# A two-layer encoder in float32 on one core: the first projection's weight groups in three rounded products instead of one float32 product, and the last chunk of each FFN in another order

## The chip, the cores and the metric

The kernel runs on one core of one Trainium2 chip. The metric is the time of one execution on the device in microseconds (us); lower is better.

## The reference

256 tokens of width 2048 go through two layers. Layer 0 mixes tokens with a convolution module, layer 1 with multi-head latent attention; each mixer is followed by a gated FFN (SwiGLU) of width 5632. All arithmetic is float32. What the change touches is the convolution module and the two FFNs:

```python
def swiglu(h, w_gate, w_up, w_down):
    return (jax.nn.silu(h @ w_gate) * (h @ w_up)) @ w_down

def conv_module(h, w_pw1, b_pw1, w_dw, b_dw, ln_g, ln_b, w_pw2, b_pw2):
    u = h @ w_pw1 + b_pw1                 # 2048 -> 4096
    a, gate = jnp.split(u, 2, axis=-1)
    v = a * jax.nn.sigmoid(gate)
    v = depthwise_causal_conv(v, w_dw, width=31) + b_dw
    v = jax.nn.silu(layernorm(v, ln_g, ln_b))
    return v @ w_pw2 + b_pw2
...
h = h + conv_module(rmsnorm(h), ...)      # layer 0; layer 1: h + mla(rmsnorm(h), ...)
h = h + swiglu(rmsnorm(h), ...)
```

## The kernel before

**Rounded products.** TensorE multiplies float32 slowly, and numbers rounded to the type fp32r fast. So a weight group (1 MB: four row tiles of 128 by 512 columns) is split in two: ScalarE writes the rounded high part `w_hi` from `raw` (`hi`, L665; `f_hi`, L793), VectorE writes the rest `w_lo = raw - w_hi` (`lo`, L981; `f_lo`, L986). The activations are split the same way into `x_hi` and `x_lo`, and a product is the sum of three: high times high, high times low, low times high (`product`, L1493).

**The rings.** `raw`, `w_hi` and `w_lo` have four slots each. A load into a `raw` slot (SyncE's queue, L485, L460, L514) waits until the low part of the slot's earlier group is made. ScalarE's high part waits until TensorE has used the slot's earlier group.

**The first projection.** It is done in eight halves; half s holds 256 value and 256 gate columns, as four groups j = 0 to 3 of four row tiles (`channel_half`, L1577). Groups 0 and 1 (`WHOLE = 2`) are multiplied in plain float32 straight from `raw`, with activations `x_f`; the load of their slot waits for TensorE itself. Groups 2 and 3 are split, but without VectorE: ScalarE writes `w_hi`, and then minus `raw`, rounded, into `w_lo` (`hi_and_negative`, L674), and a transfer issued by GpSimd adds `raw` to it (`conv_low`, L587). For the first group row of the second projection (`G_PW2` to `G_PW2 + 3`) the transfers do it too.

**What the other engines do in a half.** ScalarE takes the sigmoid of the gate (`gate_sigmoid`, L715), and multiplies 10 of the 31 taps of the convolution (`products`, L726); GpSimd sums those (`conv_sums`, L593). VectorE multiplies value and gate (L1086) and does the other 21 taps of two channel tiles, the two tiles in turn (L1096, L1101), adds GpSimd's sum (L1107) and takes row statistics (L1120). TensorE transposes the result of half s - 2 in half s (`conv_rows`, L1612). In the last half 12 taps are done by TensorE with diagonal matrices `diag_last` (L712, `conv_rows_last`, L1625); ScalarE writes these 24 matrices before half 0's sigmoid. After it come a layernorm, transposes, SiLU (`silu`, L1140) and the second projection (`square`, L1651).

**The FFN.** The hidden width is done in 11 chunks of 512. A chunk c from 1 to 10 takes 15 weight groups, in the order of L98. Seven are Strassen sums (Q1 to Q7, 12 multiplications each), four are plain (G2, G3, U2, U3, 24 each), and four (D0 to D3, 24 each) are the down projection of the chunk before. `hidden` transposes the gated activations of a chunk and splits them into `a_hi` and `a_lo`. The slot of `w_hi` and `w_lo` is the group's number modulo 4; for the last four groups, the down projection of chunk 10 (numbers 158 to 161), it is 0 to 3:

```python
def f_w(q):
    return q % RING if q < F_LAST else q - F_LAST
```

ScalarE's `f_hi` of a group waits until TensorE has used the group before it in that slot. In chunk 10 the order before is ..., D3, Q2, G2, Q4, G3, U2 (number 156), U3 (157), then `hidden(10)`, then groups 158 to 161. The order of each engine is written out by hand in `ffn(l)`: on VectorE the end of a chunk is `gate_mul(c)` (L1254), low part of the next chunk's group 0, then 1, with `up_mul(c)` (L1261) between them, 2, and `hidden(c)` (L1246).

Of the kernel before, what the change touches and what calls it, by code (L numbers as in the profile page):

```python
# [28 lines left out]
F32 = mybir.dt.float32  # L29
# [23 lines left out]
PE_TAPS_LAST = 12  # L53

# [5 lines left out]
WHOLE = 2  # L60
SPLIT = KG - WHOLE

# [16 lines left out]

G_ADDED = G_PW2 + RING  # L80
# [18 lines left out]
DOWN = (D0, D1, D2, D3)  # L99
F_CHUNK = 15  # L100
# [3 lines left out]
F_RAW = {Q1: 0, Q5: 0, Q6: 0, Q4: 0, Q3: 1, Q7: 1, D0: 4, D1: 2, D2: 3, D3: 4, Q2: 2, G2: 3, G3: 4, U2: 2, U3: 3}  # L104


def f_pos(c, p):
    return F_FIRST + F_CHUNK * (c - 1) + p


def f_part(q):
    return (q - F_FIRST) % F_CHUNK


def f_raw(q):

    if q < F_FIRST:
        return q % RING
    return F_RAW[f_part(q)] if q < F_LAST else q - F_LAST
# [61 lines left out]
def encoder(nc, x, positions, attn_norm_g, ffn_norm_g, final_norm_g, conv_w_pw1, conv_b_pw1, conv_w_dw,  # L181
# [3 lines left out]
    with ctx:  # L185
# [15 lines left out]

        with nc.sbuf_tensor("x_f", [P, WHOLE * GK, S], F32) as x_f:
            pass
# [114 lines left out]
        xf_done = sem("xf_done")  # L318
# [4 lines left out]
        glu_done = sem("glu_done")  # L323
        conv_step = sem("conv_step")
# [57 lines left out]
        def in_float32(g):  # L382
            return g < G_PW2 and g % KG < WHOLE

        def split_no(g):

            return SPLIT * (g // KG) + g % KG - WHOLE if g < G_PW2 else SPLIT * HALVES + g - G_PW2

        def wait_lo(eng, g, i=None, per=0):
            if KG <= g < G_ADDED:  # L390
                eng.wait_ge(lo_added[g % RING], 16 * (g // KG if g % KG >= WHOLE else 1))
            else:
                eng.wait_ge(lo_dve, val(split_no(g) + 1 if g < KG else SPLIT + g - G_ADDED + 1, i, per))

# [9 lines left out]
        def wait_f_used(eng, l, q):  # L404
            eng.wait_ge(f_used, F_ALL * l + q + 1)

# [23 lines left out]
        def norm_counts(n):  # L430

            return KT * n - WHOLE * GK

# [17 lines left out]
        def _(sp):  # L451
# [50 lines left out]
            def ffn_loads(l):  # L502
# [23 lines left out]
                for c in range(1, FC):  # L526
                    for p in (D3, Q2, G2):
                        part(c, p)
                    if c < FC - 1:
                        part(c + 1, Q3)  # L530
                    for p in (G3, U2, U3):
                        part(c, p)
                    if c < FC - 1:
                        part(c + 1, Q1)
                        for p in (D0, D1, D2):
                            part(c + 1, p)
                for n in range(CC):
                    f_load(F_LAST + n, w_of(l, DOWN[n], FC))
            ffn_loads(0)
# [37 lines left out]
        def _(pool):  # L577
# [9 lines left out]
            def conv_low(g):  # L587

                slot = g % RING
                pool.wait_ge(neg_done, split_no(g) - SPLIT + 1)  # L590
                pool.dma_start(hi32(w_lo[:, slot, :]), raw[:, slot, :], accum_op=ALU.add).then_inc(lo_added[slot], 16)

            def conv_sums(s):  # L593
# [3 lines left out]
                for n in range(1, PROD_TAPS[s]):  # L597
                    pool.wait_ge(prod_done, 2 * (PROD_TAP[s] + n) + 2)
# [5 lines left out]
                    if n == 2 and s < HALVES - 1:  # L604
                        conv_low(G_PW1 + KG * (s + 1) + KG - 1)
# [51 lines left out]
        def _(act):  # L657
# [44 lines left out]
            for j in range(WHOLE, KG):  # L702
                hi(G_PW1 + j)
                for k in range(GK * j, GK * j + GK, 2):
                    act.wait_ge(xt_done, k + 2 - WHOLE * GK)
# [3 lines left out]
            act.wait_ge(vec_done, 3)  # L709
            for mm in range(2):  # L710
                for w in range(PE_TAPS_LAST):
# [3 lines left out]
            def gate_sigmoid(s):  # L715

                u = s % 2
                act.wait_ge(group_used, G_PW1 + KG * s + KG)
                if s >= 2:
                    act.wait_ge(glu_done, 2 * (s - 1))  # L720
                for mm in range(2):
                    col = KT + 2 * s + mm
                    act.activation(glu_sig[:, 2 * u + mm, :], ps[:, 2 * u + 1, S * mm:S * mm + S], ACT.Sigmoid,
                                   bias=bias1_col[:, col:col + 1]).then_inc(glu_sig_done, 1)

            def products(s, n0, n1):  # L726

                u = s % 2
                for n in range(n0, min(n1, PROD_TAPS[s])):
                    w = prod_tap0(s) + n  # L730
                    if n == 0 and s >= 2:
                        act.wait_ge(conv_tr, TT * (s - 1))
                    elif n > 0 and PROD_ADD[s] + n > PROD_SLOTS:
                        act.wait_ge(prod_added, PROD_ADD[s] + n - PROD_SLOTS)
                    elif n > 0:
                        act.wait_ge(out_added, TT)
                    for mm in range(2):
                        m, tile = 2 * u + mm, 2 * s + mm
                        act.wait_ge(glu_done, tile + 1)
                        dst = acc[:, m, :] if n == 0 else prod_slot(s, n)[:, S * mm:S * mm + S]  # L740
                        act.activation(dst, vbuf[:, m, w:w + S], ACT.Copy, scale=tap_col[:, w, tile:tile + 1]
                                       ).then_inc(prod_done, 1)
# [9 lines left out]
            for s in range(HALVES):  # L752
                g = G_PW1 + KG * (s + 1)
                if s == HALVES - 1:
                    hi_and_negative(g)
                    hi_and_negative(g + 1)
                hi_and_negative(g + 2)
                gate_sigmoid(s)
                products(s, 0, 3)
                hi_and_negative(g + 3)  # L760
                if s > 0:
                    rows_out(s - 1)
                products(s, 3, TAPS)
# [50 lines left out]
            def ffn(l):  # L814

                def gate_sig(c):

                    for t in range(TT):
                        if c > 0 and t == 0:
                            act.wait_ge(tile0_done, 2 * chunk_no(l, c) + 1)  # L820
                        else:
                            wait_f_used(act, l, KG - 1 if c == 0 else f_pos(c, G3))
# [3 lines left out]
                def hidden(c):  # L826

                    for b in range(2):
                        act.wait_ge(ff_tr, 2 * (FC * l + c) + b + 1)
                        act.activation(a_hi[:, 0, 2 * b:2 * b + 2, :].rearrange("p k s -> p (k s)"), ps[:, 4 + b, :],  # L830
                                       ACT.Copy).then_inc(ahi_done, 1)

                def parts_hi(c, *parts):
                    for p in parts:
                        f_hi(l, f_pos(c, p))

# [8 lines left out]
                for c in range(1, FC):  # L845
# [4 lines left out]
                    wait_f_used(act, l, f_pos(c, Q5))  # L850
                    act.activation(q5, ps[:, 3, :], ACT.Copy).then_inc(q5_done, 1)
                    parts_hi(c, Q6, D2, Q7, D3, Q2, G2)
                    wait_f_used(act, l, f_pos(c, Q7))
                    act.activation(q167, ps[:, 1, :], ACT.Copy).then_inc(q167_done, 1)
                    parts_hi(c, Q4, G3, U2, U3)
                    parts_hi(c + 1, 0)
                    gate_sig(c)
                    if l == 1 and c == FC - 1:
                        wait_f_lo(act, l, f_pos(c, G3))
                        act.dma_start(row_bc[:, :], final_norm_g.rearrange("(a d) -> a d", a=1).to_broadcast([P, D])  # L860
                                      ).then_inc(final_g_in, 16)
                    parts_hi(c + 1, 1, 2)
                hidden(FC - 1)
                f_hi(l, F_ALL - 1)
# [107 lines left out]
        def _(dve):  # L972
# [53 lines left out]
            def first_norm(gain):  # L1026
# [17 lines left out]
                for k in range(WHOLE * GK):  # L1044
                    scaled(k, x_f[:, k, :]).then_inc(xf_done, 1)
                dve.wait_ge(sq_act, 1)
                for j in range(WHOLE, KG):
                    for k in range(GK * j, GK * j + GK):
                        scaled(k, x_t[:, S * k:S * k + S]).then_inc(xt_done, 1)
                    lo(G_PW1 + j)  # L1050
                    for k in range(GK * j, GK * j + GK, 2):
                        dve.wait_ge(xhi_done, k + 2 - WHOLE * GK)
# [4 lines left out]
                dve.tensor_copy(bias1_col[:, :], ps[:, 6, 0:2 * KT]).then_inc(vec_done, 1)  # L1057
                dve.tensor_copy(tap_col[:, :, :].rearrange("p w t -> p (w t)"), ps[:, 7, 0:TAPS * KT]).then_inc(vec_done, 1)
# [20 lines left out]
            def conv_half(s):  # L1079

                u = s % 2
                dve.wait_ge(group_used, G_PW1 + KG * s + KG)
                for mm in range(2):
                    m, tile = 2 * u + mm, 2 * s + mm
                    dve.wait_ge(glu_sig_done, tile + 1)
                    dve.scalar_tensor_tensor(vbuf[:, m, HALO:], ps[:, 2 * u, S * mm:S * mm + S],  # L1086
                                             bias1_col[:, tile:tile + 1], glu_sig[:, m, :],
                                             ALU.add, ALU.mult).then_inc(glu_done, 1)
                w0 = dve_tap0(s)
                bank = [ps[:, 6 + u, S * mm:S * mm + S] for mm in range(2)]  # L1090
                for w in range(w0, TAPS):
                    for mm in range(2):
                        m, tile = 2 * u + mm, 2 * s + mm
                        if w == w0:
                            dve.wait_ge(glu_done, tile + 1)
                            dve.tensor_scalar(bank[mm], vbuf[:, m, w:w + S], tap_col[:, w, tile:tile + 1],  # L1096
# [888 lines left out]
```

## Time and profile before

| | us |
|---|---|
| median of 3 runs (2070.03 to 2072.25) | 2071.71 |
| the profiled execution, its own time | 2071.21 |
| span of the profiled execution | 2069.4 |
| TensorE busy | 2010.9 |
| VectorE busy | 1421.9 |
| ScalarE busy | 1054.8 |
| GpSimd busy | 226.1 |

The span is what the instructions of the profile cover; the time has some 1.8 us around it. Engines are called PE (TensorE), PEld (its weight loads), DVE (VectorE), ACT (ScalarE), POOL (GpSimd) and SP (SyncE) in the profile; a q behind a name is an engine's instruction queue. PEclk is the share of full speed that TensorE's clock was granted. A float32 matmul stands in the profile as two records, a rounded one as one.

### The profile page before, as it was taken

The page shows a single profiled execution, that of the slowest core. Times are in us where ns is not written, and L with a number is a line of the kernel's source. Part 1 is how long each engine was busy: PE and PEld are TensorE (multiplying, and loading weights), DVE is VectorE, ACT ScalarE, POOL GpSimd, SP SyncE. Part 2 cuts the span into 40 slices and gives each one's busy share as a digit, 9 for nine tenths or more (in the row PEclk, how much of TensorE's full clock was granted, in tenths as well). Part 3 has the DMA queues.
Part 4 walks back from the last instruction along what each step waited for, and adds up shares of the span by engine and source line. Part 5 has one row for each costly group of instructions (what it writes and reads, how often), then busy time and mean ns, then how long its engine had stood idle before and what let it go on. Part 6 is the DMA issues. An engine that isn't in the chain of part 4 may idle for free.

```text
span 2069.4 us, 24296 instructions
## 1 busy us (share of the span) xinstructions
PE 2010.9 (97%) x9814; PEld 1705.5 (82%) x9814; DVE 1421.9 (69%) x1605; ACT 1054.8 (51%) x1020; POOL 226.1 (11%) x191
## 2 busy tenths in 40 slices
PE   8899899999999999999989999999999999999996
PEld 7898878888888888888878998888888888888885
DVE  4777676777766777667667775477766767766764
ACT  4566763545454555455445554355455445554543
POOL 0455400000000000000001000000000000000001
PEclk9999999999999999999999999999999999999998
DMA  7888946699889989898744534568988999889981
GB/s 234 240 227 234 263 143 214 169 279 258 227 224 259 268 267 236 216 260 245 243 143 138 158 122 160 191 177 270 251 217 240 253 274 262 224 227 262 263 244 61
DMA packets 254081, 457.51 MB, mean 221 GB/s; under 512 B 18452, under 2 KB 60188, under 8 KB 251164
## 3 DMA queue, kind: packets, MB, share of 16 engines
q1 hardware_dynamic: 207648, 349.73, 48.3%
q0 software_dynamic: 44832, 102.77, 28.7%
q10 hardware_dynamic: 1500, 3.61, 0.5%
q8 instruction: 71, 1.16, 0.2%
q14 instruction: 30, 0.25, 0.0%
HBM read 435.10 MB, written 2.10 MB: 211 GB/s over the span
## 4 chain that ended last, share of the span: by engine, by line
PE 85%; DVE 5%; DMA 5%; ACT 3%; issue 1%; POOL 0%; SPq 0%; ACTq 0%; DVEq 0%; POOLq 0%
PE ps L1496 82%; DVE w_lo L988 2%; DMA raw<-in_conv_w_pw_dram 2%; DMA w_lo<-raw 1%; DMA raw<-in_ffn_w_up_dram 1%; PE ps L1719 1%; POOL scratch L603 0%; PE ps L1920 0%; PE ps L1921 0%; PE ps L1901 0%; ACT w_hi L801 0%; DMA resid<-in_x_dram 0%; ACT w_lo L677 0%; ACT diag_last L712 0%; DVE x_lo L1015 0%
## 5 line engine op out<-in xcount | busy, mean ns | idle before, releaser
L988 DVE TENSOR_TENSOR w_lo<-raw,w_hi 128x2048 fp32r<-128x2048 f32 x264 | 601.5, 2287 | 279.0 <-ACT w_hi L801 278.7
L801 ACT ACTIVATE w_hi<-raw 128x2048 fp32r<-128x2048 f32 x264 | 500.9, 1914 | 488.3 <-PE ps L1496 197.1
L1496 PE MATMUL ps<-w_hi,x_hi 128*128 128x512 f32 x1328 | 517.9, 390 | 1.1 <-DVE x_lo L1015 0.9
L1496 PE MATMUL ps<-w_hi,x_lo 128*128 128x512 f32 x1328 | 516.7, 389 | 0.0
L1496 PE MATMUL ps<-w_lo,x_hi 128*128 128x512 f32 x1328 | 516.7, 389 | 0.0
L1496 PE MATMUL ps<-w_hi,a_hi 128*128 128x512 f32 (+1 forms) x768 | 294.5, 384 | 2.5 <-DVE a_lo L1250 2.5
L1496 PE MATMUL ps<-w_lo,a_hi 128*128 128x512 f32 (+1 forms) x768 | 293.9, 383 | 0.0
L1496 PEld LDWEIGHTS ps<-w_hi,x_hi 128*128 128x128 f32 x1328 | 249.3, 188 | 53.9 <-DVE x_lo L1015 1.4
L1496 PE MATMUL ps<-w_hi,a_lo 128*128 128x512 f32 (+1 forms) x768 | 293.6, 382 | 0.0
L1496 PEld LDWEIGHTS ps<-w_hi,x_lo 128*128 128x128 f32 x1328 | 249.3, 188 | 52.1
L1496 PEld LDWEIGHTS ps<-w_lo,x_hi 128*128 128x128 f32 x1328 | 249.3, 188 | 51.3
L622 POOL DMA_DIRECT2D raw<-in_ffn_w_up_dram x60 | 77.1, 1285 | 1255.1 <-DVE w_lo L988 1255.1
L672 ACT ACTIVATE w_hi<-raw 128x2048 fp32r<-128x2048 f32 x73 | 138.5, 1910 | 147.8 <-PE ps L1496 74.3
L1496 PEld LDWEIGHTS ps<-w_hi,a_hi 128*128 128x128 f32 x768 | 145.6, 190 | 31.7 <-DVE w_lo L988 3.5
L1496 PEld LDWEIGHTS ps<-w_hi,a_lo 128*128 128x128 f32 x768 | 145.6, 190 | 28.0
L1496 PEld LDWEIGHTS ps<-w_lo,a_hi 128*128 128x128 f32 x768 | 145.6, 190 | 27.7
L801 ACT ACTIVATE w_hi<-row_bc 128x2048 fp32r<-128x2048 f32 x60 | 115.2, 1919 | 92.7 <-PE ps L1496 92.7
L983 DVE TENSOR_TENSOR w_lo<-raw,w_hi 128x2048 fp32r<-128x2048 f32 x55 | 125.5, 2291 | 40.8 <-ACT w_hi L672 40.6
L988 DVE TENSOR_TENSOR w_lo<-row_bc,w_hi 128x2048 fp32r<-128x2048 f32 x60 | 137.0, 2284 | 4.6 <-ACT w_hi L801 4.5
L1496 PE MATMUL ps<-w_hi,s_hi 128*128 128x512 f32 x320 | 126.4, 395 | 0.0
L1496 PE MATMUL ps<-w_hi,s_lo 128*128 128x512 f32 x320 | 124.8, 390 | 0.0
L1496 PE MATMUL ps<-w_lo,s_hi 128*128 128x512 f32 x320 | 124.5, 389 | 0.0
(210 smaller groups left out, 2323.8 us busy)
## 6 DMA issues: line engine op xcount, KB each, us to landing
raw<-in_ffn_w_gate_dram SPq DMA_DIRECT2D x68, 1024.0 KB, 9.5
raw<-in_ffn_w_up_dram SPq DMA_DIRECT2D x68, 1024.0 KB, 7.5
raw<-in_ffn_w_up_dram POOLq DMA_DIRECT2D x60, 1024.0 KB, 9.0
raw<-in_ffn_w_down_dram SPq DMA_DIRECT2D x48, 1024.0 KB, 6.0
row_bc<-in_ffn_w_down_dram SPq DMA_DIRECT2D x40, 1024.0 KB, 8.8
raw<-in_conv_w_pw_dram SPq DMA_DIRECT2D x64, 512.0 KB
raw<-in_ffn_w_gate_dram POOLq DMA_DIRECT2D x20, 1024.0 KB, 9.8
row_bc<-in_ffn_w_gate_dram SPq DMA_DIRECT2D x20, 1024.0 KB, 6.4
```

The source lines that it names most:

```text
L622: pool.dma_start(f_raw_tile(l, q).rearrange("p (k n) -> p k n", k=GK), w_of(l, p, c), accum_op=ALU.add).then_inc(f_added[f_raw(q)], 16)
L672: act.activation(w_hi[:, slot, :], raw[:, slot, :], ACT.Copy).then_inc(hi_done, 1)
L801: act.activation(f_w_tile(w_hi, l, q), f_raw_tile(l, q), ACT.Copy).then_inc(f_hi_done, 1)
L983: dve.tensor_tensor(w_lo[:, g % RING, :], raw[:, g % RING, :], hi32(w_hi[:, g % RING, :]), ALU.subtract).then_inc(lo_dve, 1)
L988: dve.tensor_tensor(f_w_tile(w_lo, l, q), f_raw_tile(l, q), hi32(f_w_tile(w_hi, l, q)), ALU.subtract).then_inc(f_lo_done, 1)
L1496: ins = pe.matmul(dst, lhsT, rhs, start=first and n == 0, stop=last and n == len(pairs) - 1, skip_group_check=skip)
L1719: ins = pe.transpose(ps[:, 4 + b, S * kk + P * t:S * kk + P * t + P], ff_h[:, t, P * m:P * m + P], ident[:, :])
```

## The change

- All groups of the first projection but group 0 of half 0 are now split. In each half from 1 on, the low parts of groups 0 and 1 are made by VectorE and those of groups 2 and 3 by transfers, as before (`ADDED_FROM = 2`). Loads into the slots of groups 0 and 1 now wait for the low part and not for TensorE. `x_hi` and `x_lo` are made for all 16 row tiles, in the order of groups 1, 2, 3, 0.
- The low parts of `G_PW2` to `G_PW2 + 3` are made by VectorE: one before `silu(0)`, three inside the SiLU loop.
- ScalarE writes the diagonal matrices four per half in halves 1 to 6, and a small sigmoid early.
- GpSimd issues both transfers of a half before it starts its sums.
- In half 7 groups 2 and 3 are multiplied for channel tile 0 first and then for tile 1; sigmoid, taps and products are done for tile 0 and then for tile 1, no longer in turn.
- In chunk 10 of each FFN, D2 and D3 move behind U3, with `hidden(10)` between them; Q2 stands before Q7, and Q4 behind G3. `hidden(10)` has its own slot of `a_hi` and `a_lo` and uses PSUM banks 0 and 1.

```diff
-WHOLE = 2
-SPLIT = KG - WHOLE
+FIRST_ORDER = (1, 2, 3, 0)
+ADDED_FROM = 2
...
+ORDER_LAST = (Q1, Q3, Q5, D0, D1, Q6, Q2, Q7, G2, G3, Q4, U2, U3, D2, D3)
...
 def f_pos(c, p):
-    return F_FIRST + F_CHUNK * (c - 1) + p
+    return F_FIRST + F_CHUNK * (c - 1) + (ORDER if c < FC - 1 else ORDER_LAST).index(p)
...
         def in_float32(g):
-            return g < G_PW2 and g % KG < WHOLE
+            return g == G_PW1
...
@@ GpSimd
             for s in range(HALVES):
-                if s == HALVES - 1:
-                    for j in range(WHOLE):
-                        conv_low(G_PW2 + j)
-                    conv_low(G_PW2 + WHOLE)
-                else:
-                    conv_low(G_PW1 + KG * (s + 1) + WHOLE)
+                if s < HALVES - 1:
+                    for j in range(ADDED_FROM, KG):
+                        conv_low(G_PW1 + KG * (s + 1) + j)
                 conv_sums(s)
-            conv_low(G_PW2 + KG - 1)
...
@@ ScalarE, a half
+            for s in range(HALVES - 1):
+                g = G_PW1 + KG * (s + 1)
+                hi(g + 1)
+                hi_and_negative(g + 2)
+                for mm in range(2):
+                    gate_sigmoid(s, mm)
+                hi_and_negative(g + 3)
+                products(s, 0, 3)
+                if s > 0:
+                    rows_out(s - 1)
+                products(s, 3, PROD_TAPS[s])
+                if s < HALVES - 2:
+                    hi(g + KG)
+                if s > 0:
+                    last_diagonals(s - 1)
...
@@ VectorE, a half but the last
+                    gated(0)
+                    gated(1)
+                    lo(G_PW1 + KG * (s + 1) + 1)
+                    for w in range(w0, TAPS):
+                        tap(w, 0)
+                        tap(w, 1)
+                    if s < HALVES - 2:
+                        lo(G_PW1 + KG * (s + 2))
...
@@ ScalarE, chunk 10
+                        parts_hi(c, G3, Q4, U2, U3)
+                        gate_sig(c)
+                        parts_hi(c, D2, D3)
+                        f_hi(l, f_next(c, 0))
...
+                    f_hi(l, f_next(c, 1))
...
                 hidden(FC - 1)
-                f_hi(l, F_ALL - 1)
+                for n in (2, 3):
+                    f_hi(l, F_LAST + n)
...
@@ VectorE, chunk 10
+                        gate_mul(c)
+                        parts_lo(c, D2, D3)
+                        f_lo(l, f_next(c, 0))
+                        up_mul(c)
+                        f_lo(l, f_next(c, 1))
+                        hidden(c)
+                        add(2, f_pos(c, D2))
+                        f_lo(l, f_next(c, 2))
...
@@ TensorE, chunk 10
                     plain(c, U2, 2, 2)
                     plain(c, U3, 2, 3)
+                    if c == FC - 1:
+                        down(c - 1, 2, f_pos(c, D2))
+                        hidden(c)
+                        down(c - 1, 3, f_pos(c, D3))
...
-                        if block_no >= 2:
+                        if block_no >= 2 or c == FC - 1:
                             pe.wait_ge(out_added, added + TT * CC * c + block_no - 3)
```

## Rows read from the trace of the kernel before

**Rows 1.** The page: the chain that ended last, share of the span by line.

```profile
PE ps L1496 82%; DVE w_lo L988 2%; DMA raw<-in_conv_w_pw_dram 2%; DMA w_lo<-raw 1%; DMA raw<-in_ffn_w_up_dram 1%; PE ps L1719 1%; POOL scratch L603 0%; PE ps L1920 0%; PE ps L1921 0%; PE ps L1901 0%; ACT w_hi L801 0%; DMA resid<-in_x_dram 0%; ACT w_lo L677 0%; ACT diag_last L712 0%; DVE x_lo L1015 0%
```

**Rows 2.** Windows, by stage: length, engines' busy us, granted clock, transfers' busy share, GB/s.

```profile
43.10:77.40 34.30, 28.02 (x162) 25.81 (x161) 18.19 (x46) 23.77 (x38) 14.33 (x12) 0.90 0.70 185
...
155.80:181.70 25.90, 25.90 (x166) 24.03 (x165) 18.86 (x48) 16.78 (x28) 13.31 (x11) 1.00 0.93 242
181.70:211.20 29.50, 27.53 (x167) 25.62 (x165) 18.86 (x48) 18.28 (x29) 13.28 (x11) 0.94 0.90 240
...
1043.70:1054.00 10.30, 7.00 (x20) 5.57 (x21) 8.01 (x7) 3.47 (x4) 0.00 (x0) 0.50 0.66 217
```

**Rows 3.** TensorE's timeline in the halves: start, duration, records, idle time before.

```profile
31.00 0.28 PE L1496 MATMUL ps<-x_lo,w_hi 128*128 128x256 f32 x1
...
36.39 0.28 PE L1496 MATMUL ps<-x_lo,w_hi 128*128 128x256 f32 x1
...
69.40 0.58 PE L1496 MATMUL ps<-x_hi,w_hi 128*128 128x256 f32 x1 [4.82 <-DMA w_lo<-raw]
...
129.68 7.07 PE L1496 MATMUL ps<-x_f,raw 128*128 128x256 f32 x32
162.67 0.60 PE L1621 MATMUL ps<-ident,scratch 128*128 128x128 f32 x4
...
203.85 0.43 PE L1496 MATMUL ps<-x_hi,w_hi 128*128 128x256 f32 x1 [1.97 <-DMA w_lo<-raw]
```

**Rows 4.** The half from 129.7 to 155.8, instructions by line and shape.

```profile
L1101 DVE SCALAR_TENSOR_TENSOR ps<-scratch,tap_col,ps 128x256 f32<-128x256 f32 x40 | 15.8, 483 | 0.0
...
L603 POOL TENSOR_TENSOR scratch<-scratch,row_bc 128x512 f32<-128x512 f32 x9 | 11.6, 1286 | 2.9 <-ACT row_bc L741 1.9
...
L672 ACT ACTIVATE w_hi<-raw 128x2048 fp32r<-128x2048 f32 x2 | 3.8, 1904 | 9.5 <-DMA raw<-in_conv_w_pw_dram 9.5
```

**Rows 5.** Transfers in the half from 155.8 to 181.7, by queue (q1 loads, q0 the additions).

```profile
GB/s 350 348 346 98 3 8 0 0 202 202 202 202 202 202 202 101 101 55 345 387 369 389 302 215 240 215 202 215 234 136 378 383 383 354 350 353 343 359 350 361
...
q1 hardware_dynamic: 4174, 4.14, 48.5%
q0 software_dynamic: 288, 2.10, 43.6%
```

**Rows 6.** VectorE's timeline ahead of half 0 and in the SiLU loop.

```profile
38.38 4.49 DVE L1075 TENSOR_TENSOR resid<-resid,row_bc 128x2048 f32<-128x2048 f32 x2
...
266.89 0.69 DVE L1144 TENSOR_TENSOR scratch<-scratch 128x512 f32<-128x512 f32 x1 [2.74 <-ACT scratch L784]
```

**Rows 7.** TensorE's timeline behind the last half.

```profile
241.21 12.58 PE L1496 MATMUL ps<-diag_last,scratch 128*128 128x128 f32 x96 [3.65 <-DVE scratch L1086]
257.32 1.16 PE L1496 MATMUL ps<-ident,scratch 128*128 128x128 f32 x8 [3.53 <-DVE scratch L1107]
...
269.90 0.47 PE L1496 MATMUL ps<-w_hi,x_hi 128*128 128x512 f32 x1 [0.20 <-DVE x_lo L1152]
```

**Rows 8.** The chain at the end of the first FFN.

```profile
1034.93 5.45 PE ps L1496 x24
...
1040.47 1.92 ACT w_hi L801
...
1044.62 1.40 DVE scratch L1268 x2
...
1048.97 13.52 PE ps L1496 x48
```

**Rows 9.** VectorE in chunk 10 of the first FFN, around Q6 and Q7.

```profile
1002.69 0.69 DVE L1304 TENSOR_TENSOR scratch<-scratch,ps 128x512 f32<-128x512 f32 x1
1003.41 0.70 DVE L1306 TENSOR_TENSOR ps<-ps,scratch 128x512 f32<-128x512 f32 x1
```

**Rows 10.** GpSimd's issue of a transfer, beside VectorE idle and beside a low part.

```profile
398.98 1.29 POOL L622 DMA_DIRECT2D raw<-in_ffn_w_up_dram  x1 [1.94 <-DVE w_lo L988]
...
472.44 1.28 POOL L622 DMA_DIRECT2D raw<-in_ffn_w_up_dram  x1 [7.73 <-DVE w_lo L988]
```

More of the change, by code:

```diff
@@ L118, in f_raw @@
         return q % RING
[L119 removed]
+    if q >= F_LAST:
+        return q - F_LAST
+    return (F_RAW_LAST if in_last(q) else F_RAW)[f_part(q)]
 def f_w(q):
@@ L708, in _, with last_diagonals @@
             act.dma_start(row_bc[:, :], conv_b_pw2[0:1, :].to_broadcast([P, D])).then_inc(bias2_in, 16)
-            act.wait_ge(vec_done, 3)
-            for mm in range(2):
-                for w in range(PE_TAPS_LAST):
+            act.activation(esum[:, 0:1], ident[:, 0:1], ACT.Sigmoid).then_inc(warm, 1)
+            def last_diagonals(part):
+                for n in range(part * DIAG_PART, (part + 1) * DIAG_PART):
+                    w, mm = n // 2, n % 2
                     act.activation(diag_last[:, mm, w, :], ident[:, :], ACT.Copy,
@@ L744, in rows_out @@
+            def products(s, n0, n1):
+                for n in range(n0, n1):
+                    for mm in range(2):
+                        product_of(s, n, mm)
             def rows_out(s):
@@ L1089, in conv_half @@
[L1089 to L1102 removed]
+                last = s == HALVES - 1
@@ new lines, in conv_half, with gated @@
+                w0 = dve_tap0(s)
+                steps = TAPS - w0
+                bank = [ps[:, 6 + u, S * mm:S * mm + S] for mm in range(2)]
+                def gated(mm):
+                    tile = 2 * s + mm
+                    dve.wait_ge(glu_sig_done, tile + 1)
+                    dve.scalar_tensor_tensor(vbuf[:, 2 * u + mm, HALO:], ps[:, 2 * u + mm, 0:S],
+                                             bias1_col[:, tile:tile + 1], glu_sig[:, 2 * u + mm, :],
+                                             ALU.add, ALU.mult).then_inc(glu_done, 1)
@@ new lines, in tap @@
+                def tap(w, mm):
+                    m, tile = 2 * u + mm, 2 * s + mm
+                    if w == w0:
+                        dve.wait_ge(glu_done, tile + 1)
+                        dve.tensor_scalar(bank[mm], vbuf[:, m, w:w + S], tap_col[:, w, tile:tile + 1],
+                                          vec_col[:, R_BDW + tile:R_BDW + tile + 1],
+                                          ALU.mult, ALU.add).then_inc(conv_step, 1)
+                        return
+                    dve.wait_ge(conv_step, DVE_STEP[s] + (steps * mm + w - w0 if last else 2 * (w - w0) + mm - 1))
+                    dve.scalar_tensor_tensor(bank[mm], vbuf[:, m, w:w + S], tap_col[:, w, tile:tile + 1],
+                                             bank[mm], ALU.mult, ALU.add).then_inc(conv_step, 1)
@@ new lines, in conv_half @@
+                if last:
+                    for mm in range(2):
+                        gated(mm)
+                        for w in range(w0, TAPS):
+                            tap(w, mm)
+                else:
+                    gated(0)
+                    gated(1)
+                    lo(G_PW1 + KG * (s + 1) + 1)
+                    for w in range(w0, TAPS):
+                        tap(w, 0)
+                        tap(w, 1)
+                    if s < HALVES - 2:
+                        lo(G_PW1 + KG * (s + 2))
@@ L1584, in channel_half @@
                     g = G_PW1 + KG * s + j
-                    if j < WHOLE:
+                    if in_float32(g):
                         pe.wait_ge(raw_in[g % RING], LANDED * (g // RING + 1))
-                        w = w_rows(raw, g % RING)
                     else:
                         wait_lo(pe, g)
-                        wh, wl = w_rows(w_hi, g % RING), w_rows(w_lo, g % RING)
-                    if s == 0 and j < WHOLE:
-                        pe.wait_ge(xf_done, GK * (j + 1))
+                    if s == 0 and j == 0:
+                        pe.wait_ge(xt_done, GK)
@@ new lines, in channel_products @@
+            def channel_products(s, j, tiles):
+                slot = (G_PW1 + KG * s + j) % RING
+                w, wh, wl = w_rows(raw, slot), w_rows(w_hi, slot), w_rows(w_lo, slot)
+                for kk in range(GK):
+                    k = GK * j + kk
+                    for m in tiles:
+                        cols = slice(P * m, P * m + P)
+                        if in_float32(G_PW1 + KG * s + j):
+                            pairs = [(w[:, kk, cols], x_t[:, S * k:S * k + S])]
+                        else:
+                            pairs = [(wh[:, kk, cols], x_hi[:, k, :]), (wh[:, kk, cols], x_lo[:, k, :]),
+                                     (wl[:, kk, cols], x_hi[:, k, :])]
+                        ins = product(ps[:, 2 * (s % 2) + m % 2, S * (m // 2):S * (m // 2) + S], pairs,
+                                      k == 0 and m < 2, k == KT - 1, skip=True)
+                return ins
```

343 lines of the change are left out of this document (198 added, 145 removed).

## The prediction

> **What bounds it now.** I read the page first, for where the time is: TensorE is busy 2010.9 us of 2069.4 (the table), and 82% of the chain that ended last is its multiplications [rows 1]. So a change pays only where it takes work from TensorE or a gap out of its row. Then I read the windows by stage [rows 2], TensorE's timeline [rows 3, 7] and the chain around each gap [rows 8].
>
> In the halves of the first projection TensorE hardly waits: the half from 155.8 lasts 25.9 us, the clock is granted in full, and transfers are busy 93% beside it. A float32 group is 32 records in 7.07 us [rows 3]. A rounded one is 48 multiplications; 45 of them start between 31.00 and 36.39, 0.12 us each, so 5.76 us [rows 3]. Two of each and the transposes of 0.6 make 26.2. Two halves stand out: the one from 43.1 takes 34.3, the one from 181.7 takes 29.5 [rows 2]; both wait for a transfer into `w_lo` (4.82 and 1.97 us) [rows 3] and then run at a lower clock. Behind the last half TensorE idles 3.65 us, does the diagonal taps in 12.6, idles again, and starts the second projection at 269.9 [rows 7].
>
> At each FFN's end U3 stops at 1040.4. The chain goes on over ScalarE's high part of group 159, VectorE's low part and `up_mul` to 1046.0, and the next multiplication starts at 1048.97 [rows 8]. The clock is at 0.50 from 1043.7 to 1054.0, so 48 multiplications take 13.5 us [rows 2, 8].
>
> **The change, part by part.**
>
> *Half 0.* One float32 group becomes rounded: 7.07 to 5.76, so half 1 begins at 43.1 - 1.2 = 41.9. The low parts of groups 1, 2, 3 lie under group 0's multiplications.
>
> *Half 1.* Its floor is four groups, 23.05 us, against 34.3. The long wait goes: ScalarE no longer writes 24 matrices ahead of the rounded copies, and transfers are issued before the sums. VectorE gets later: the row it adds to the residual is requested behind one more high part. Its 4.49 us of adds began at 38.4 [rows 6]; I take 40.1 (38.4 to 42 are the ends), so it takes up half 0 at 44.6. The low part of group 8 comes 21.8 later (18.86 less 1.5 of adds and statistics, plus two low parts of 2.2; DVE's busy time of [rows 2]), at 66.4, while TensorE wants it at 41.9 + 23.05 = 64.95. Half 2 begins at 66.5, before at 77.4.
>
> *Halves 2 to 7.* TensorE's floor is 4 x 5.76 + 0.6 = 23.65. The others come close. VectorE: 18.86 [rows 2] + 2 x 2.2 = 23.3. ScalarE: 16.78 [rows 2] + two high parts of 1.8 (1904 ns, overlapping by 0.1) [rows 4] + four matrices of 0.3 = 21.6. Transfers: (48.5% + 43.6%) of 25.9 = 23.9 [rows 5], 24.1 with the bytes that slid into the next half. GpSimd's nine sums of 1.29 [rows 4] have room. So transfers become the tightest. What orders them: a load waits until the earlier addition in its slot has landed, the addition waits for ScalarE's two copies of the group, and ScalarE stands in order with the sigmoid. I follow one half from its start at 0: additions issued at about 0 and 5.6 (sigmoids 0.9, two copies 3.7, issue 0.9), loads behind low parts at -1 and 4, the other two loads behind the additions. The queue is never empty as long as an addition ends before the load queued beside it. Bounds for a half are 23.65 (nothing late) and 26 (2 us of idle transfers, if both end together). I take 24.4: 24.1 and 0.3 for starts. Half 7 ends at 66.5 + 6 x 24.4 = 212.9, before at 241.21 - 3.65 = 237.6 [rows 7]: **-24.7 us**.
>
> *Behind half 7.* The taps of a tile now follow one another, and each reads what the one before wrote. In turn, 40 take 15.8 us, 0.39 each, at a duration of 0.48 [rows 4]. Dependent steps of 0.69 start 0.72 apart [rows 9], so a dependent tap costs 0.51, and 14 of them 7.2. VectorE is free of half 6 just before half 7 ends (0), finishes tile 0 at 7.3, gates tile 1, and is through at 15.1, with the adds at 15.9. TensorE's diagonal taps (12.6) and GpSimd's four sums end by then. Before, the same matmuls started 257.32 - 237.56 = 19.8 behind the half [rows 7]: **-3.9**. The low parts in the SiLU loop: the first fits into the idle 2.74 [rows 6]; the one behind block 0 makes block 1 some 1.2 later, of which TensorE feels **+0.5**. Bounds 0 and +3.
>
> *FFN, chunk 10, middle.* Q7 needs `mix_q1_q6`, which had D2's 5.44 us as cover and now has Q2's 2.7. VectorE's queue put its second step at 1002.7 [rows 9]; it ends at 1003.4, and TensorE is there at 1002.3: 1.1, and 0.2 for G2's low part behind it. **+1.3** per layer.
>
> *FFN, chunk 10, end.* One would read D2 and D3 as cover for the gaps before and behind `hidden(10)`. But look at who holds the slots of `w_hi`. Groups 158 and 159 have slots 0 and 1, as numbers 156 and 157 do. These were U2 and U3; now they are D2 and D3. ScalarE's high part of 158 waits until D2 is used, VectorE makes its low part *before* `up_mul`, and the transposes wait for `up_mul`. So behind D2 stands the same chain as before behind U3: 1.9 + 2.2 + 1.4, 5.7 us of idle [rows 8]. Then D3 runs, and the high part of 159, ahead of ScalarE's copy into `a_hi`, waits until D3 is used. Behind D3: high part 1.9, low part 2.2, two `a_lo` 1.2, and the first residual add of D2 0.6, because block 0 now waits for it: 6.0 us of idle. The clock falls 3.3 us into a gap and is back 10.3 later [rows 2, 8]. Taken over as it stands here, the first gap, transposes and D3 take 16.1 us for 6.3 of work (9.8 lost), the second loses 6.0 and 7.5 us at half speed, 9.8. Together 19.6, with the middle 20.9. Before: from 1040.4 to 1062.5 22.1 us for 11.8 of work [rows 8], 10.3 lost. So +10.6 per layer, **+21.2** in both. Bounds: +12 for both if the clock falls once only, +24.
>
> Sum: -24.7 - 3.9 + 0.5 + 21.2 = -6.9. The profiled execution's time is 2071.2 (span 2069.4 and 1.8 around it), 0.5 under the median: 2064.3 for it, 2064.8 for the median. I say **2065 us**.
>
> **Rivals.**
> 1. *Transfers set the halves.* If loads and additions share the engines so that both end together, the next load leaves them idle for some 2 us and a half takes 25.7 to 26. In [rows 5] the second addition runs beside a load at 302 to 389 GB/s for five slices and then alone at some 215, so they do mix. Six halves at 26 instead of 24.4 give 2065 + 9.6 = 2074.6, no change. From 26.4 a half on, it is slower. That point is reached if waits of 2 us as at 203.85 [rows 3] come back, each with its half clock: a half of 27 gives 2081. For it: VectorE, ScalarE and transfers all above 88% of the half. Against: both waits of before came from a late issue, which is now early. [...]
> 2. *The FFN ends are covered after all* (I misread the slots): both lose only the 1.3 in the middle. -2 x 9.0 instead of +21.2: 2026.
> 3. *The clock falls once per FFN end* or the second gap is half as long: +12 instead of +21: 2056.
>
> **Chances.** My forecast, 2059 to 2069: 0.50. Rival 1: 0.27, of which 0.14 within 0.2% (4.1 us, about what a measurement of this kernel can tell) and 0.13 slower. Rival 2: 0.07. Rival 3: 0.16. Of my forecast some 0.06 lies within 4.1 us of before. Faster 0.67, same 0.20, slower 0.13. The range leaves out rival 2 and the far end of rival 1: 2054 to 2077.
>
> **What would show it.** Half 1 has no wait of 4.8 us, and half 2 begins near 66.5. Halves 2 to 6 are 24 to 25 us apart; waits in them are for `w_lo<-raw`. The matmuls of the last conv rows start some 16 us behind half 7. In each FFN two gaps near 6 us stand around D3, the first ended by `up_mul`, the second by VectorE, and the granted clock falls twice. Wrong would be: no gap behind D2 (rival 2), or halves above 25.5 (rival 1).

## The result and the profile after

The changed kernel takes 2059.38 us (median of 5 runs, 2054.65 to 2062.48); the kernel before took 2070.73 (5 runs, 2069.95 to 2072.25). The ratio is 0.9936, with a 95% interval of 0.9920 to 0.9952: 0.64% faster. The profiled execution took 2054.65 us, the fastest of the five, with a span of 2052.8; before it was 2069.4, so the two traces differ by 16.6 us where the medians differ by 11.4. The runs also scatter more than before, 7.8 us against 2.3.

Where the 16.6 us are, from the two traces: the second projection of the convolution module ends at 328.66 instead of 357.20 (-28.5); from there to the residual transposes at the first FFN's end it is 710.88 us instead of 705.28 (+5.6); the attention part keeps its 281.0; the rest, with the second FFN, grows from 725.9 to 732.25 (+6.35).

**The halves.** Windows over the halves, cut at about their starts, columns as in [rows 2]:

```profile
42.00:66.00 24.00, 21.79 (x180) 21.38 (x179) 24.00 (x49) 20.07 (x29) 13.51 (x11) 1.00 0.94 240
65.00:89.00 24.00, 23.57 (x197) 23.36 (x196) 22.78 (x49) 21.28 (x35) 13.38 (x11) 1.00 0.97 262
...
137.50:161.50 24.00, 23.63 (x197) 23.43 (x197) 23.01 (x51) 21.89 (x35) 13.39 (x11) 1.00 0.98 264
...
186.00:206.50 20.50, 17.30 (x145) 17.09 (x143) 19.11 (x45) 17.14 (x32) 12.19 (x11) 1.00 0.98 256
```

The half from 43.1, 34.3 us in [rows 2], is now some 24, and the transfers have gone from 0.93 to 0.98 of a half. The sigmoids of halves 1 and 6 start at 67.95 and 188.75, five halves at 24.16. What repeats from one half to the next is seen in the chain, one turn of it (start, duration, what):

```profile
77.05 0.39 SPq L510
...
77.48 11.24 DMA raw<-in_conv_w_pw_dram
...
88.77 1.80 issue
90.57 1.90 ACT w_lo L705
92.47 0.29 issue
92.76 8.26 DMA w_lo<-raw
...
101.04 0.39 SPq L510
```

A load lands, ScalarE makes the high part and the negative copy, the addition lands, and only then the next load of that slot is issued: 23.99 us, 19.5 of them two transfers. TensorE is not in it. A share of 0.98 does not mean that the transfers never pause. The half from 137.5 to 161.5 in 40 slices of 0.6 us:

```profile
GB/s 367 215 22 43 131 328 384 387 432 316 218 218 218 191 205 205 205 15 225 377 374 333 425 299 205 196 201 241 246 242 203 171 348 369 386 362 213 271 379 382
```

At 22 and 43 GB/s (138.7 to 139.9) the load has landed and ScalarE still makes the copies, up to 140.60, that the addition waits for. Behind the last half the chain reads:

```profile
193.51 12.99 DMA w_lo<-raw
...
206.54 10.38 PE ps L1603 x72
216.91 0.44 PE ps L1743 x4
217.35 10.72 PE ps L1603 x96
...
228.10 0.72 PE ps L1603 x4
```

The last addition needs 13 us from issue to landing and TensorE waits 3.24 for it; behind this wait the clock is at 0.50 for 3.4 us (207.3 to 210.7). Half 7 ends at 216.9, and the last matmuls of the convolution rows start 11.2 us behind it, right behind the diagonal taps.

**The FFN's end.** TensorE's waits in the whole kernel (line, releaser: us in total, times, longest), and the chain at the end of the first FFN, which answers to [rows 8]:

```profile
PE ps L1603 <- DVE resid L1365: 12.5, 2, 6.2
PE ps L1844 <- DVE scratch L1357: 11.4, 2, 5.7
PE ps L1642 <- DMA resid<-in_x_dram: 8.1, 2, 5.9
PE ps L1603 <- DMA w_lo<-raw: 7.6, 6, 3.2
```

```profile
969.97 36.87 PE ps L1603 x161
...
1006.91 1.92 ACT w_hi L850
...
1009.00 2.07 issue
1011.07 1.41 DVE scratch L1357 x2
...
1012.52 1.97 PE ps L1844 x8
1014.49 6.35 PE ps L1603 x24
...
1020.92 1.92 ACT w_hi L850
...
1022.86 2.29 DVE w_lo L1054
1025.16 1.20 DVE a_lo L1339 x2
1026.35 0.60 DVE resid L1365
...
1027.05 12.49 PE ps L1603 x48
```

The gap of 5.7 us behind U3 has become a gap of 5.7 behind D2, and a second one of 6.2 stands behind D3, step by step as forecast. The clock does not follow the forecast. Windows, column PEclk:

```profile
1009.40:1016.30 6.90, 3.78 (x13) 3.39 (x14) 3.07 (x3) 0.00 (x0) 0.00 (x0) 0.51 0.46 152
1016.30:1023.10 6.80, 4.52 (x20) 3.40 (x19) 0.24 (x1) 2.18 (x2) 0.00 (x0) 1.00 0.00 0
1023.10:1029.90 6.80, 2.85 (x7) 2.30 (x8) 6.80 (x7) 4.30 (x4) 0.00 (x0) 0.50 0.44 154
```

It falls twice, to 1.2 of 2.4 GHz, but is back after 6.8 us each time, in [rows 2] after 10.3.

### The profile page after: what moved, and what is told of

Same layout as the page of the kernel before. It is cut to its first block, busy times and chain, and to the rows that moved or that the text cites. A ratio compares the mean times of both kernels' runs of the same rounds, so it can differ in the third digit from the quotient of the medians.

```text
span 2052.8 us, 24901 instructions
## 1 busy us (share of the span) xinstructions
PE 1991.1 (97%) x10054; PEld 1696.8 (83%) x10054; DVE 1468.4 (72%) x1628; ACT 1078.4 (53%) x1036; POOL 223.5 (11%) x187
## 4 chain that ended last, share of the span: by engine, by line
PE 83%; DMA 8%; DVE 4%; ACT 2%; issue 2%; SPq 0%; POOL 0%; ACTq 0%; DVEq 0%; POOLq 0%
PE ps L1603 80%; DMA raw<-in_conv_w_pw_dram 4%; DMA w_lo<-raw 3%; DVE w_lo L1054 2%; PE ps L1844 1%; DMA raw<-in_ffn_w_up_dram 1%; ACT w_lo L705 1%; ACT w_hi L850 1%; PE ps L2066 0%; PE ps L2067 0%; PE ps L2047 0%; DMA resid<-in_x_dram 0%; SPq L510 0%; PE ps L1653 0%; DVE w_lo L1049 0%
## 5 line engine op out<-in xcount | busy, mean ns | idle before, releaser
L1054 DVE TENSOR_TENSOR w_lo<-raw,w_hi 128x2048 fp32r<-128x2048 f32 x264 | 601.6, 2288 | 290.2 <-ACT w_hi L850 289.8
L850 ACT ACTIVATE w_hi<-raw 128x2048 fp32r<-128x2048 f32 x264 | 500.6, 1915 | 482.8 <-PE ps L1603 218.8
L700 ACT ACTIVATE w_hi<-raw 128x2048 fp32r<-128x2048 f32 x88 | 167.0, 1912 | 95.0 <-PE ps L1603 73.2
L1049 DVE TENSOR_TENSOR w_lo<-raw,w_hi 128x2048 fp32r<-128x2048 f32 x74 | 169.0, 2290 | 40.9 <-ACT w_hi L700 40.6
L1603 PEld LDWEIGHTS ps<-w_hi,a_lo 128*128 128x128 f32 x768 | 145.8, 190 | 28.1
L1603 PE MATMUL ps<-x_hi,w_hi 128*128 128x256 f32 (+1 forms) x512 | 147.1, 287 | 7.6 <-DMA w_lo<-raw 7.6
L1603 PE MATMUL ps<-x_hi,w_lo 128*128 128x256 f32 (+1 forms) x512 | 145.5, 284 | 0.0
L1603 PE MATMUL ps<-x_lo,w_hi 128*128 128x256 f32 (+1 forms) x512 | 145.4, 284 | 0.0
```

The costliest lines, as they stand in the source:

```text
L700: act.activation(w_hi[:, slot, :], raw[:, slot, :], ACT.Copy).then_inc(hi_done, 1)
L850: act.activation(f_w_tile(w_hi, l, q), f_raw_tile(l, q), ACT.Copy).then_inc(f_hi_done, 1)
L1049: dve.tensor_tensor(w_lo[:, g % RING, :], raw[:, g % RING, :], hi32(w_hi[:, g % RING, :]), ALU.subtract).then_inc(lo_dve, 1)
L1054: dve.tensor_tensor(f_w_tile(w_lo, l, q), f_raw_tile(l, q), hi32(f_w_tile(w_hi, l, q)), ALU.subtract).then_inc(f_lo_done, 1)
L1603: ins = pe.matmul(dst, lhsT, rhs, start=first and n == 0, stop=last and n == len(pairs) - 1, skip_group_check=skip)
```

## The experiments

Eleven kernels ran. The kernel before had a median of 2071.3 us beside the first four, 2073.0 beside the next four and 2071.6 beside the last three (9 runs each), so kernels of different groups are compared with up to 2 us of doubt.

**Each part alone.** The first kernel has the whole change but its FFN part; the second has the FFN part only.

> The changed kernel with the order of chunk 10 of both FFNs as before (D2 and D3 in front, one hidden(10) behind U3). Theory: the FFN part of the change costs 5.6 us in layer 0 and 6.4 in layer 1 (the profiles before and after, from the end of the second projection or of the output projection on), so this is 12 us faster than the changed kernel: 2047 (ratio to before 0.9886). If the forecast's size of 21 were right and the profile after lucky, 2038. Rival, the FFN part helps and the profile misleads: above 2059.

> The kernel before with only the new order of chunk 10 of both FFNs. Theory: two gaps near 6 us per layer in place of one, 12 us slower than before: 2083. With the clock low for 10.3 us behind each gap, as forecast: 2092. Rival, D2 and D3 cover the gaps: 2053.

Measured: 2044.22 us (2042.25 to 2045.14), ratio 0.9864 [0.9849, 0.9879], and 2084.63 (2084.28 to 2089.78), ratio 1.0069 [1.0055, 1.0082]. The first projection gives 27.1 us, 3 more than expected (2047), and the FFN part takes 13.4 back; together they make 13.7 us faster, between the 11.4 of the medians and the 16.6 of the spans. Taken between the first kernel and the changed one, the FFN part costs 15.2 us in the medians; the traces before and after give 12.0. The FFN part alone makes the kernel slower, and both gaps are in its trace at the same sizes as in the changed kernel:

```profile
PE ps L1563 <- DVE resid L1325: 12.5, 2, 6.2
PE ps L1789 <- DVE scratch L1317: 11.4, 2, 5.7
```

The first of these kernels also bears on the length of the low clock, for its two FFN ends are the same instructions in the same order, each with a gap of 5.7 us, as in the kernel before. Windows of it:

```profile
1020.80:1027.60 6.80, 4.76 (x15) 3.82 (x16) 5.71 (x6) 2.99 (x3) 0.00 (x0) 0.50 0.78 237
1027.60:1037.30 9.70, 9.70 (x45) 7.97 (x44) 4.62 (x4) 1.92 (x1) 0.00 (x0) 1.00 0.48 161
2003.80:2014.10 10.30, 6.33 (x18) 5.04 (x19) 8.68 (x7) 4.14 (x4) 0.00 (x0) 0.50 0.00 0
```

One end has 6.8 us at the low clock, the other 10.3. The length is not fixed by the gap and the instructions around it, then: the same ones come with either.

**Which wait makes the two gaps.** The third kernel moves one line on VectorE, the fourth covers both gaps:

```diff
 parts_lo(c, D2, D3)
-f_lo(l, f_next(c, 0))
 up_mul(c)
+f_lo(l, f_next(c, 0))
 f_lo(l, f_next(c, 1))
```

```diff
 # VectorE
 parts_lo(c, D2, D3)
-f_lo(l, f_next(c, 0))
 up_mul(c)
-f_lo(l, f_next(c, 1))
+f_lo(l, f_next(c, 0))
 hidden(c)
 add(2, f_pos(c, D2))
+f_lo(l, f_next(c, 1))
 f_lo(l, f_next(c, 2))
 # ScalarE
-    f_hi(l, f_next(c, 1))
     if c < FC - 1:
+        f_hi(l, f_next(c, 1))
         f_hi(l, f_next(c, 2))
 hidden(FC - 1)
-for n in (2, 3):
+for n in (1, 2, 3):
     f_hi(l, F_LAST + n)
```

> The changed kernel; on VectorE in chunk 10 up_mul now stands in front of the low part of group 158. Theory of the slots: the first gap of each layer (5.7 us, slow transposes 1.1, low clock in D3 0.9) goes, the one behind D3 stays: 2 x 7.7 = 15 us less than the changed kernel, 2044. Rival, the gap is due to up_mul's own wait for U3 or to the transposes: no change, 2059.

> As the run with up_mul first, and on ScalarE and VectorE hidden(10) stands in front of group 159's high and low part (VectorE: up_mul, low part of 158, hidden, adds of D2, low parts of 159 and 160). Theory: both gaps go and the clock stays up in both layers, 2 x 15.5 = 31 us less than the changed kernel: 2028. Rival, the second gap only moves (low part of 159 late, D(10, 1) waits 4 us): 2036. Rival, loads of groups 158 to 161 are late: above 2040.

Measured: 2043.51 us (2039.92 to 2045.07), ratio 0.9861 [0.9845, 0.9876], and 2029.31 (2028.13 to 2034.18), ratio 0.9799 [0.9786, 0.9813]. So the first gap of both layers is worth 16 us and the second 14, each with its stretch at the low clock. In the fourth kernel the same place reads, in the chain:

```profile
1010.14 0.87 PE ps L1844 x8
1011.02 5.47 PE ps L1603 x24
...
1016.57 1.93 ACT w_hi L850
...
1018.52 4.49 DVE w_lo L1054 x2
1023.01 0.61 DVE resid L1365
...
1023.75 5.71 PE ps L1603 x24
1029.47 0.87 PE ps L1653 x8
```

The transposes take 0.87 us instead of 1.97, the multiplications 5.47 instead of 6.35, and of both gaps one wait of 1.7 us remains, ahead of the last 24, at the full clock. This version beats both kernels: 30 us under the changed one, 42 under the one before. The experiments below start from it, and "the covered version" is this one.

**What sets the halves.** Half the bytes of each addition, and 6 of VectorE's 21 taps left out:

```diff
-pool.dma_start(hi32(w_lo[:, slot, :]), raw[:, slot, :], accum_op=ALU.add)
+pool.dma_start(hi32(w_lo[:, slot, 0:GK * CH // 2]), raw[:, slot, 0:GK * CH // 2], accum_op=ALU.add)
```

```diff
 def dve_tap0(s):
-    return prod_tap0(s) + PROD_TAPS[s]
+    return prod_tap0(s) + PROD_TAPS[s] + (6 if s < HALVES - 1 else 0)
```

> The version with both FFN ends covered, but each adding transfer of the first projection moves only the first half of its columns (the other half of those low parts stays the negative copy, so the product is wrong there). VectorE, ScalarE, GpSimd and TensorE have the same work. Theory (transfers set halves 2 to 7): the halves fall from 24.2 to TensorE's own 23.65 us, 3.3 us in six halves, and the wait of 5.0 us in half 7 goes, of which VectorE, 3.1 us ahead there, lets through 3.1: 2029.3 - 6.4 = 2023, bounds 2020 and 2026; the waits of TensorE for w_lo<-raw fall from 8.7 us to under 2. Rival (VectorE or ScalarE sets the halves, the transfers only end last by chance): 2028 to 2031, halves still 24.2 apart.

> The version with both FFN ends covered, but VectorE leaves out 6 of its 21 taps for each of the two tiles of halves 0 to 6 (those terms of the depthwise convolution are missing): 12 x 0.39 = 4.7 us less for VectorE in each half. Theory (transfers set the halves, VectorE only follows): 2029, bounds 2027 and 2031, halves 24.0 to 24.5 apart, the additions and their waits where they were. Rival (VectorE, at 22.4 to 23.1 of 24 us, sets the halves, through the low parts that free the slots for the loads): 2023 or less, halves at 23.65.

Measured: 2020.68 us (2019.62 to 2022.70), ratio 0.9752 [0.9736, 0.9768], and 2027.77 (2027.62 to 2032.51), ratio 0.9790 [0.9773, 0.9807]. The same half in either:

```profile
137.50:161.50 24.00, 24.00 (x202) 24.00 (x202) 23.71 (x52) 22.11 (x35) 13.39 (x11) 1.00 0.80 225
```

```profile
137.50:161.50 24.00, 23.54 (x196) 23.34 (x196) 18.66 (x38) 21.57 (x34) 15.31 (x12) 1.00 1.00 263
```

With half the additions TensorE is never idle in it and the halves are 23.52 us apart (sigmoids at 65.52 and 183.14), against 24.35 in the covered version. With VectorE at 18.7 of 24 us they are 24.14 apart, where the changed kernel, with all its taps, has 24.16: nothing gained, and the time is the covered version's within the doubt between groups. Transfers set the halves, VectorE does not. ScalarE's two copies are in the same loop (some 4 us of the 24) and no run shortens them, so how much of a half they hold is not shown. The first result is 8.6 us under the covered version where 6.4 was expected: 0.83 us per half came, not 0.55, since four groups need 23.5 us of TensorE and not 23.65.

**The wait in half 7.** In the covered version it is 5.0 us. The low part of the last group goes to VectorE, after 7 of its taps:

```diff
 for w in range(w0, TAPS):
     tap(w, 0)
     tap(w, 1)
+    if s == HALVES - 2 and w == w0 + 6:
+        lo(G_PW2 - 1)
```

> The version with both FFN ends covered, and the low part of the last group of half 7 made by VectorE after 7 of its taps instead of by the adding transfer that landed 13.9 us after its issue. TensorE's wait of 5.0 us in half 7 goes. Theory (VectorE is next in line): its taps of half 6 end 2.2 us later, so of its 3.1 us of idle time 0.9 is left to gain: the last matmuls of the convolution rows start at 229.3, before 230.2, and the time is 2028.4, bounds 2027 and 2031. Rival (the wait is worth its 5.0 us and the half clock behind it, 1.7): 2022 to 2024.

Measured: 2029.02 us (2027.11 to 2031.13), ratio 0.9791 [0.9774, 0.9807]: no gain, as the theory had it. TensorE's wait of 5.0 us for the addition is gone. In its place TensorE waits 2.5 us for VectorE ahead of and among the transposes and the diagonal taps, and 2.4 us ahead of the last matmuls, which start at 229.8 instead of 230.2.

**The order of the last taps.** The last half's 28 taps alternate again between the tiles:

```diff
-for mm in range(2):
-    gated(mm)
-    for w in range(w0, TAPS):
-        tap(w, mm)
+gated(0)
+gated(1)
+for w in range(w0, TAPS):
+    tap(w, 0)
+    tap(w, 1)
```

> The version with both FFN ends covered, but VectorE's 28 taps of half 7 alternate between the two tiles again, both gated first, while TensorE and ScalarE keep the order tile by tile. Theory: the taps start when tile 1 is there (219.5 instead of 214.3) and take 28 x 0.39 = 10.9 us instead of two times 7.3 and a gate: the adds end near 231.5 instead of 230.2, and the time is 2030.8, bounds 2029 and 2032. Rival (tile by tile is worth the 3.9 us that the prediction gave to the stretch behind half 7): 2033 or more.

Measured: 2029.90 us (2029.21 to 2031.53), ratio 0.9794 [0.9779, 0.9810]. That is the covered version's time within its scatter: tile by tile is worth at most 1 to 2 us there. In the trace the last matmuls start at 230.4, 12.8 behind the half (217.6), against 11.2 in the covered version.

**What removed the long wait of half 1.** The matrices go back ahead of half 0's copies; or the second addition goes back behind two sums:

```diff
+for part in range(HALVES - 2):
+    last_diagonals(part)
 for s in range(HALVES - 1):
     g = G_PW1 + KG * (s + 1)
     hi(g + 1)
 ...
-    if s > 0:
-        last_diagonals(s - 1)
```

```diff
 # in conv_sums, behind each sum
+if n == 2 and s < HALVES - 1:
+    conv_low(G_PW1 + KG * (s + 1) + KG - 1)
 ...
-for j in range(ADDED_FROM, KG):
+for j in range(ADDED_FROM, KG - 1):
     conv_low(G_PW1 + KG * (s + 1) + j)
```

> The version with both FFN ends covered, but ScalarE writes the 24 diagonal matrices of the last half ahead of half 0's copies, as the kernel before did, instead of four per half. 24 x 0.3 = 7.3 us on ScalarE near 35, of which 2.2 fall into its idle time: the two additions of half 1 are issued some 5 us later. Theory (the long wait in half 1 came from these matrices): since the halves behind follow a transfer loop that has no slack, the 5 us stay: 2034, bounds 2032 and 2036, with a wait for w_lo<-raw of 4 to 6 us in half 1. Rival (the order of the issues was what removed that wait, and the queue hides the matrices): 2028 to 2030.

> The version with both FFN ends covered, but GpSimd issues the second addition of each half behind its first two sums, as the kernel before did, instead of ahead of them. The sums wait for ScalarE's products, so the issue moves from some 2 us to some 5 us behind the sigmoids. Theory (the queue is full anyway: the second addition's first packet goes 6 us behind its issue, when the first addition is through): 2029 to 2031. Rival (each half follows the issue): 3 us in each of seven halves, 2040 to 2050.

Measured: 2035.72 us (2034.13 to 2038.61), ratio 0.9829 [0.9816, 0.9843], and 2037.81 (2032.54 to 2038.35), ratio 0.9825 [0.9810, 0.9839]. The matrices cost 6 us that no later half gives back. But TensorE does not wait for an addition as expected:

```profile
PE ps L1604 <- DVE w_lo L1050: 6.3, 1, 6.3
```

It is VectorE's low part of half 1's second group, whose high part stands on ScalarE behind the matrices. With the late issue neither theory holds: 8.5 us, in place of 0 to 2 or of 20. The queue is not full enough to hide it:

```profile
91.33 0.87 POOL L625 DMA_DIRECT2D w_lo<-raw  x1 [3.89 <-ACT w_lo L707]
101.64 0.88 POOL L625 DMA_DIRECT2D w_lo<-raw  x1
```

The second issue comes 10.3 us behind the first (4.3 in the covered version), 6 later and not the 3 I had taken, because each of the two sums waits for ScalarE's products. TensorE's waits for `w_lo<-raw` grow from 8.7 to 18.4 us. The trace is of this kernel's slowest execution, 2038.35 us.

Where the two lose their time tells them apart. The sigmoids behind half 1 start at 67.51 in the covered version, at 74.76 with the matrices first and at 67.85 with the late issue (77.61 in the kernel before). So the matrices cost 7.3 us by the end of half 1. The late issue costs 0.3 there, but from then on its halves are 25.85 us apart instead of 24.35, and its wait in half 7 is 6.6 instead of 5.0.

**Three by VectorE, one by transfer.**

```diff
-ADDED_FROM = 2
+ADDED_FROM = 3
 ...
-hi_and_negative(g + 2)
+hi(g + 2)
 ...
     tap(w, 0)
     tap(w, 1)
+    if w == w0 + 6:
+        lo(G_PW1 + KG * (s + 1) + 2)
```

> The version with both FFN ends covered, but VectorE makes three of the four low parts of each half and only one comes by an adding transfer. The transfers lose one addition of some 5 us per half, VectorE gets 2.2 us more: 23.0 + 2.2 = 25.2 us per half against 24.2 now. Theory: VectorE now sets the halves, 7 x 1.0 to 1.3 us later in all, and the 5.0 us wait of half 7 turns into VectorE's: 2035, bounds 2031 and 2038. Rival (fewer transfers are worth more than VectorE's time, since VectorE also waited): 2021 to 2026.

Measured: 2037.79 us (2035.41 to 2040.52), ratio 0.9836 [0.9822, 0.9850]. The same half:

```profile
137.50:161.50 24.00, 22.06 (x182) 21.65 (x182) 24.00 (x47) 17.83 (x29) 12.62 (x10) 1.00 0.71 191
```

VectorE is busy without a break, transfers 71%, and the halves are 25.7 us apart. Two and two is the better split of the two tried.

## Why the prediction was right, and where it was off

**Halves 1 to 7.** Right in the size of a half. The forecast had 24.4 us a half from the transfers; they took 24.16. It got the size from the busy time of all transfers (24.1) and named the waits that order them; in the trace these waits are a loop of one slot, load, copies and addition (23.99), in which the transfers pause. That the two sums are alike was in part luck: a later issue of one addition, with the same bytes, made the halves 25.85. That the transfers and not VectorE close it was argued from 24.1 against 23.3 us, and is shown by the half additions (23.52 us a half) and the fewer taps (24.14). The end of half 7 came at 216.9 instead of 212.9. Of these 4.0 us half 1 has 1.4: half 2 begins at 67.9, not 66.5, and what TensorE waited for in half 1 was an addition (2.18 us), not VectorE's low part, which the forecast had made the last to come. The five halves behind it give 1.2 back. Half 7 takes 28.2 instead of 24.4, with the wait of 3.24 for the last addition, which lands beside loads of the second projection, and 3.4 us at the low clock.

**Behind half 7.** The dependent taps take 0.52 us (6.79 for 13), forecast 0.51. The stretch is 11.2 us and not 16, but this is no further gain: while TensorE waited in half 7, VectorE caught up. VectorE is through with the adds at 228.1, forecast 228.8, so here the forecast had the engine that ends last right. Removing TensorE's wait alone brought nothing. The two errors (-20.7 instead of -24.7, and -8.6 instead of -3.9) cancel for that reason: the second projection ends 28.5 us earlier, forecast 28.1.

**Half 1's reason.** The prediction named two for the end of half 1's long wait, the matrices and the order of the issues. By the end of half 1 the matrices alone are worth 7.3 us and the order of the issues 0.3; the order pays later, 1.5 us in each half. Before, that point stood another 2.9 us later; these are not separated. Neither kernel brings the wait of 4.8 us for an addition in half 1 back, so what made that wait is shown only in part.

**FFN, middle.** Forecast +1.3 per layer, in the trace +0.4 in the first layer and nothing in the second.

**FFN, end: the term that was mis-sized.** The prediction read the slots rightly and gave both gaps and what ends them: 5.7 and 6.0 us, in the trace 5.7 and 6.2. It then priced the clock "as it stands here", 10.3 us at half speed behind each gap, and came to +10.6 per layer with the middle. Measured are +5.6 in the first layer and +6.35 in the second, so 12.0 instead of 21.2. Each gap's low clock lasted 6.8 us. So in the first layer the first gap, transposes and D3 take 14.0 us for 6.3 of work, 7.7 lost, and from D3's end to the residual transposes it is 18.7 for 10.9, 7.8 lost; the forecast had 9.8 for each. The rival that was nearest, +12 because the clock falls once only or the second gap is half as long, gives the number but not the reason: the clock falls twice and both gaps are full.

**The rivals.** Transfers do set the halves, but at 24.2, not 26. VectorE's new low parts and GpSimd's sums could also hold each other up. In the changed kernel this does not show: both low parts stand where no sum runs. It shows once a low part stands among the taps (below). The FFN ends were not covered; the time that rival 2 gave for covered ends was 2026, and the version in which they are covered measures 2029.

**Between the median and the span.** The forecast for the median was 2065, with 2059 to 2069 as its own range; 2059.4 is inside by 0.4 us, and that is luck. For the profiled execution it was 2064.3, and 2054.65 came: of these 9.6 us the FFN term is 9.2. That execution is the fastest of five. Only one execution has a trace, so why the others are slower is not shown. Longer stretches at the low clock do not explain all of it: the execution of 2060.43 us has a mean granted clock of 0.990, the one of 2054.65 us 0.989.

## What to carry to other kernels

When work is moved in front of a gap to cover it, list who holds the buffer slots that the next loads and copies need, and in which order each engine issues: here one moved line (the multiplication that the transposes wait for ahead of a low part that nobody waits for yet) gave 16 us, more than the 11 of the change itself, and with the second gap covered too it was 30. When a stage is a loop over buffers (load, copy, add, load again), its period is that loop's, here 19.5 us of transfers in 24.0. Less work on an engine outside the loop did not change it (24.14); half the bytes of the additions did (23.52, then TensorE's own time), and so did a later issue (25.85). Price the low clock behind a gap as a range from the stretches that the trace has, never as one number.

## What the hardware showed unexpectedly

**The length of the low clock.** In the traces of these kernels the stretches behind gaps are 3.4, 6.8 or 10.2 us long, if the kernel's end does not cut them off (six in the kernel before, among them 3.4 at 204 and 10.2 at 1043.7), and the same instructions with the same 5.7 us gap had 6.8 in one layer and 10.2 in the next. What decides between them was not found. In the traces at hand all ten stretches at FFN ends in the new order (four in the changed kernel, four in the one with the FFN part only, two in the one with `up_mul` first) are 6.8, and three of the four in the old order are 10.2, so a part of the order in it is not excluded.

**VectorE and GpSimd in each other's way.** In the kernel where VectorE makes the last low part among its taps, its timeline and GpSimd's read:

```profile
198.23 2.98 DVE L1051 TENSOR_TENSOR w_lo<-raw,w_hi 128x2048 fp32r<-128x2048 f32 x1
```

```profile
197.76 1.30 POOL L640 TENSOR_TENSOR scratch<-scratch,row_bc 128x512 f32<-128x512 f32 x1
```

```profile
199.21 3.16 POOL L640 TENSOR_TENSOR scratch<-scratch,row_bc 128x512 f32<-128x512 f32 x1
```

The low part starts 0.8 us before a sum ends and takes 2.98 us instead of 2.28; the next sum starts beside it, takes 3.16 instead of 1.30, and ends at 202.37, 1.2 us behind the low part. So each waits for the end of the other's instruction. The Trainium skill ("SBUF — State Buffer", section "SBUF: two separate sides") has this as an exclusive lock between GpSimd and a VectorE operation with two SBUF inputs; this trace agrees. VectorE's taps, which read one operand from PSUM, leave the sums at 1.30. With three low parts by VectorE it came in five of the seven halves (2.9 to 3.3 us for the low part among the taps, 0.6 to 1.0 more than alone), enough for the 0.5 us by which 25.7 exceeds the forecast 25.2.
